# Odd attention scores as three fp32r products, and one LayerNorm's vectors loaded later

## The chip, the cores and the metric

The kernel runs on one core of a Trainium2 chip. The metric is the time of one execution on the device, in microseconds. TensorE (PE) multiplies, VectorE (DVE), ScalarE (ACT) and GpSimd (POOL) do the elementwise work, SyncE (SP) issues most transfers. Each engine takes its instructions in the order of its own queue and waits on semaphores for the others. Two formats of a matmul's operands occur here: fp32, whose two records in the trace are one instruction in the program, and fp32r, one record for each instruction, which rounds its operands.

## What is computed

A decoder trunk of two layers over 512 tokens of width 1024. Each layer is a mixer and a gated feed-forward network with a causal convolution of width 3, each followed by LayerNorm over `alpha * x + f(x)`. Layer 0 has the even mixer (16 heads of width 64), layer 1 the odd one (8 stick-breaking heads of width 128). The change touches the odd mixer:

```python
q, k, v = split_heads(h, w_qkv, 8, 128)          # h @ w_qkv
z = (q * 128 ** -0.5) @ k.T                      # per head, 128 queries at a time
z = where(kpos < t, z, -inf)
sp = max(z, 0) + log1p(exp(-abs(z)))
r = sum of sp from each key to the last          # reversed cumulative sum
out = exp(z - r) @ v
x = layer_norm(alpha * x + merge_heads(out) @ w_o, ln_mix_g, ln_mix_b)
```

## The kernel before

All large products run as three fp32r matmuls: an operand `w` is kept as a head `w_hi` (rounded to fp32r) and a rest `w_lo = w - w_hi`, and hi·hi, hi·lo and lo·hi are summed in PSUM. ACT writes the heads (L447 for the streamed weights), POOL (L311) and DVE the rests. Weights stream in 1 MB steps into two buffers `w_raw`.

The odd attention goes over eight positions, one head each (`odd_position` on PE, `odd_body` on ACT and DVE, `odd_position` on POOL). In position i the four query tiles j of 128 rows take the keys of tiles 0 to j, so scores are 128, 256, 384 and 512 columns wide. For a tile, PE writes z to bank 2 or 3 (`scores`, L1455), DVE masks the diagonal (L1048), ACT computes `log1p(exp(-abs(z)))` (L570 to L574), DVE adds the maximum, scans in reverse and subtracts (L1055, L1060, L1063: `break_stick`), ACT takes the exponential (L579), PE transposes (L1465), DVE (tiles 0 and 2, L977) or ACT (tiles 1 and 3, L482) copies the transposed weights out, and PE multiplies by the values (`weigh`, L1476).

Between these PE runs the projection of the next head's q and k, in its queue at places written by hand: `share = (10, 11, 15, 8, 2)` matmuls of 128x512 before tile 0's transposes, before tile 1's, before tile 2's, before tile 3's, and after the next position's first scores. 24 matmuls project one head's q into bank 0, 24 its k into bank 1. `EARLY` puts the first 12 of q for the position after the next behind those for the next one. So in a position i of 0 to 5 the first 36 matmuls finish q and k of head i+1, and what `fill(3)`, the share of 8 before tile 3's transposes, takes is the start of q of head i+2. It writes bank 0, in which q of head i+1 stood, and so waits:

```python
pe.wait_ge(a["q_ok" if l else "q_cp"], c + 2 * it)   # project_early, l = 1
```

`q_ok` counts the heads whose q has been read out of bank 0. Before the change ACT reads it in one copy (L592, scaled, into `qa`) and counts `q_ok`; the same for k (L598, `ka`, `k_ok`). PE waits for both again before the first scores of the next position. Positions 6 and 7 have no such early share.

DVE's body of a position ends with `turn_out(a, 2, ...)`, the copy L977 of tile 2's transposed weights. ACT loads gain and shift of a LayerNorm (`load_gain`, L451, two DMAs on its queue): for the even mixer right behind its attention, for the odd mixer at the end of layer 0's last LayerNorm, behind a wait for all of its rows. VectorE waits for them (`gb_full`) before the first row tile of the LayerNorm.

Of the kernel before, what the change touches and what calls it, by code (L numbers as in the profile page):

```python
# [22 lines left out]
F32 = mybir.dt.float32  # L23
F32R = mybir.dt.float32r
ACT = mybir.ActivationFunctionType
ALU = mybir.AluOpType

P = 128
S, D, DEPTH = 512, 1024, 2
# [3 lines left out]
NT = S // P  # L33
# [4 lines left out]
SB_SCALE = 128 ** -0.5  # L38
# [42 lines left out]
def build(nc, x_in, w_stream, ident_in, rope_in, mask_in, tri_in, conv_in, ln_in, out):  # L81
    ctx = ExitStack()
    with ctx:
        def sb(name, shape, dt=F32, stack=ctx):
            return stack.enter_context(nc.sbuf_tensor(name, shape, dt))
# [36 lines left out]
        with ExitStack() as st:  # L122
            v_all = sb("v_all", [P, NT, D], stack=st)
            v_pos = [sb(f"v_pos{s}", [P, NT, P], stack=st) for s in range(2)]
            probs_t = [sb(f"probs_t{h}", [P, NT, S], stack=st) for h in range(2)]
            with ExitStack() as ev:
                qa_hi = [sb(f"qa_hi{s}", [P, S], F32R, stack=ev) for s in range(2)]
                ka_hi = [sb(f"ka_hi{s}", [P, S], F32R, stack=ev) for s in range(2)]
            qa = [sb(f"qa{s}", [P, S], stack=st) for s in range(2)]
            ka = [sb(f"ka{s}", [P, S], stack=st) for s in range(2)]  # L130
            probs = [[sb(f"probs{h}{s}", [P, S], stack=st) for s in range(2)] for h in range(2)]
            with ExitStack() as ev:
                rope = sb("rope", [P, 2, S], stack=ev)
                masks = sb("masks", [P, 2, S], stack=ev)
                qc = sb("qc", [P, S], stack=ev)
                qs = sb("qs", [P, S], stack=ev)
                kc = sb("kc", [P, S], stack=ev)
                ks = sb("ks", [P, S], stack=ev)
                sm = sb("sm", [P, 2, 2, 4], stack=ev)
            with ExitStack() as od:  # L140
                soft = [sb(f"soft{s}", [P, S], stack=od) for s in range(2)]
                tri = sb("tri", [P, P], stack=od)
# [47 lines left out]
        class Phase:  # L190
# [4 lines left out]
            def __getitem__(self, n):  # L195
# [4 lines left out]
        V = [Phase(f"v{l}", "rows act dve") for l in range(DEPTH)]  # L200
        both = "q_mm q_ok k_ok s_mm p_ok t_mm tev_a tev_v v_pos pv ot_hi ot_lo "
        A = [Phase("a0", both + "q_cp k_cp q_sw k_sw q_m k_m s_rd ex rc p_ok1"),
             Phase("a1", both + "zm ab e1 ln sp sc rr")]
        N = [Phase(f"n{i}", "rows sum mean sq lv y0 va nt mulg xn") for i in range(2 * DEPTH)]
        T = [Phase(f"t{i}", "mm hi lo") for i in range(2 * DEPTH)]

# [235 lines left out]
        def _(act):  # L442
# [119 lines left out]
            def odd_body(b, c, it, dense, before, early):  # L562
                a = A[1]
                i = c + 2 * it

                def soft_part(j):
                    g, L = 4 * i + j, (j + 1) * P
                    e = soft[j % 2][:, 0:L]
                    act.wait_ge(a["zm"], g + 1)
                    act.activation(e, bank[2 + j % 2][:, 0:L], ACT.Abs).then_inc(a["ab"], 1)  # L570
                    act.wait_ge(a["ab"], g + 1)
                    act.activation(e, e, ACT.Exp, scale=-1.0).then_inc(a["e1"], 1)
                    act.wait_ge(a["e1"], g + 1)
                    act.activation(e, e, ACT.Ln, bias=1.0).then_inc(a["ln"], 1)  # L574

                def weight_part(j):
                    g, L = 4 * i + j, (j + 1) * P
                    act.wait_ge(a["rr"], g + 1)
                    act.activation(probs[0][j % 2][:, 0:L], probs[0][j % 2][:, 0:L], ACT.Exp).then_inc(a["p_ok"], 1)  # L579

                soft_part(0)
                soft_part(1)
                weight_part(0)
                heads(b + AT_QK + c + 2, it)
                if before:
                    out_heads(a, i - 1, (c - 1) % 2)
                weight_part(1)
                soft_part(2)
                turn_out(a, 1, 4 * i + 1, dense)
                if dense:  # L590
                    act.wait_ge(a["q_mm"], i + 2)
                    act.activation(qa[(c + 1) % 2][:, :], bank[0][:, :], ACT.Copy,  # L592
                                   scale=SB_SCALE).then_inc(a["q_ok"], 1)
                soft_part(3)
                weight_part(2)
                if dense:
                    act.wait_ge(w_used, b + AT_QK + i + 2)
                    act.activation(ka[(c + 1) % 2][:, :], bank[1][:, :], ACT.Copy).then_inc(a["k_ok"], 1)  # L598
                weight_part(3)
                turn_out(a, 3, 4 * i + 3, dense)  # L600

# [13 lines left out]
            for l in range(DEPTH):  # L615
                b = l * PER_LAYER

                if l == 0:
                    a = A[0]
                    query_copied(0)  # L620
                    act.wait_ge(w_used, b + 1)
                    act.activation(kc[:, :], bank[1][:, :], ACT.Copy).then_inc(a["k_cp"], 1)
                    body = even_body
                else:
                    a = A[1]

                    act.wait_ge(a["q_mm"], 1)
                    act.activation(qa[0][:, :], bank[0][:, :], ACT.Copy, scale=SB_SCALE).then_inc(a["q_ok"], 1)
                    act.wait_ge(w_used, b + 1)
                    act.activation(ka[0][:, :], bank[1][:, :], ACT.Copy).then_inc(a["k_ok"], 1)  # L630
                    act.dma_start(tri[:, :], tri_in).then_inc(tri_full, 16)
                    body = odd_body

# [19 lines left out]
                        body(b, 1, it, True, True, True)  # L653
                        body(b, 2, it, True, True, True)
                body(b, 7, 0, False, True, False)
                if l == 0:
                    load_gain(0)
                out_heads(A[l], 7, 1)

                for c in range(2):  # L660
# [3 lines left out]
                for i, after in ((2 * l, b + AT_O + 4), (2 * l + 1, b + PER_LAYER)):  # L664
# [167 lines left out]
                    else:  # L832
# [14 lines left out]
                            act.wait_ge(w_used, after)  # L847
                            act.activation(w_hi[s][:, part], w_raw[first % 2][:, 0:Q], ACT.Copy).then_inc(w["hi"], 1)
                        xt_heads(i + 1, 3)
                        if i % 2:  # L850
                            act.wait_ge(N[i]["xn"], NT)
                            load_gain(i + 1)


        @block.vector
        def _(dve):
# [130 lines left out]
            def even_body(c, it, dense, before, kind):  # L987
# [51 lines left out]
                if dense:  # L1039
                    k_rest(a, (c + 1) % 2, i + 1)  # L1040

            def odd_body(c, it, dense, before, kind):
                a, i = A[1], c + 2 * it

# [29 lines left out]
                break_stick(2)  # L1074
                break_stick(3)
                turn_out(a, 2, 0, 4, 4 * i + 2)

            dve.memset(v_all[:, 0, 0:P], 1.0).then_inc(warm_ready, 1)
            dve.memset(eps[:, :], 4 * EPS).then_inc(set_ready, 1)
# [9 lines left out]
            for l in range(DEPTH):  # L1089
                if l == 0:  # L1090
                    a = A[0]
                    dve.wait_ge(even_full, 32)
                    rope_k_cos(a, 0, 0)
                    rope_k_sin(a, 0, 0)
                    k_rest(a, 0, 0)
                    body = even_body
                else:
                    dve.wait_ge(tri_full, 16)
                    body = odd_body
                for t in range(NT):  # L1100
# [169 lines left out]
        def _(pe):  # L1270
# [171 lines left out]
            def odd_position(b, c, it, dense, early=False, filler=(), first=False):  # L1442
# [9 lines left out]
                        next(more, None)  # L1452

                def scores(j, p=par):
                    pe.matmul(bank[2 + j % 2][:, 0:(j + 1) * P], qa[p][:, j * P:(j + 1) * P],  # L1455
                              ka[p][:, 0:(j + 1) * P], start=True, stop=True).then_inc(a["s_mm"], 1)

                def turn(j):
                    pe.wait_ge(a["p_ok"], 4 * i + j + 1)
# [290 lines left out]
```

## Time and profile before

| | us |
|---|---|
| median of 3 runs | 1203.4 (1203.36 to 1203.89) |
| the profiled execution | 1203.59 |
| its span, first to last instruction | 1201.8 |
| PE busy | 1176.5 (98%) |
| DVE busy | 717.7 (60%) |
| ACT busy | 636.6 (53%) |
| POOL busy | 691.4 (58%) |

The odd attention lies between 676 and 809 us of the span; a position in its middle takes 16.52 us. A matmul's recorded duration includes its way through the array, and matmuls overlap: the time that one costs is the distance to the next. The chain of waits adds such distances up, and is the view to read them from.

### The profile page before, as it was taken

Reading aid. Unit: us, or ns where it says so; the run is one execution under the profiler, and the core shown is the slowest. Engines: PE = TensorE matmul, PEld = TensorE weight load, DVE = VectorE, ACT = ScalarE, POOL = GpSimd, SP = SyncE. Lnnn points to the kernel's source line nnn. Section 1 sums busy time; section 2 is a strip of 40 time slices with the busy share of each in tenths; the row PEclk is TensorE's granted clock in tenths of the full one; section 3 lists DMA queues with packets and bytes.
Section 4 is the critical chain, followed back from the end, with each engine's and each line's share of the span. In section 5 each row is a group of like instructions: output and inputs, shape, how many; then the busy total and the mean of one; then the engine's idle time right before and its main releaser. Section 6 shows DMA issues by size and latency. Waiting matters only on the chain.

```text
span 1201.8 us, 19742 instructions
## 1 busy us (share of the span) xinstructions
PE 1176.5 (98%) x7458; PEld 1038.3 (86%) x7458; DVE 717.7 (60%) x1376; ACT 636.6 (53%) x1105; POOL 691.4 (58%) x426
## 2 busy tenths in 40 slices
PE   9999998999999999999999999999999999999996
PEld 9877776789999999888788788878999999998885
DVE  2135556279988888421380455654998888872226
ACT  3256666355766666422242476753676666652223
POOL 4545555157877777654624333225687777765443
PEclk9999999999999999999999999999999999999999
DMA  6322212222232223422332211212122323243211
GB/s 252 124 76 74 97 62 96 73 103 71 106 105 105 105 105 105 143 103 105 103 107 101 77 54 52 70 70 105 36 106 105 105 105 105 105 140 105 105 70 70
DMA packets 20040, 117.42 MB, mean 98 GB/s; under 512 B 2448, under 2 KB 2832, under 8 KB 7568
## 3 DMA queue, kind: packets, MB, share of 16 engines
q1 hardware_dynamic: 18400, 112.21, 26.0%
q10 hardware_dynamic: 1584, 4.51, 1.2%
q8 instruction: 30, 0.49, 0.2%
q14 instruction: 26, 0.21, 0.1%
HBM read 110.41 MB, written 2.10 MB: 94 GB/s over the span
## 4 chain that ended last, share of the span: by engine, by line
PE 87%; DVE 7%; ACT 2%; POOL 2%; issue 1%; DVEq 0%; ACTq 0%
PE bank L1606 33%; PE bank L1302 29%; PE bank L1333 15%; POOL w_lo L311 2%; PE bank L1401 2%; PE bank L1476 1%; PE bank L1455 1%; PE bank L1415 1%; PE bank L1387 1%; PE bank L1277 1%; ACT w_hi L447 1%; PE bank L1465 1%; DVE ln_mul L893 1%; DVE x L873 1%; DVE xt_lo L861 1%
## 5 line engine op out<-in xcount | busy, mean ns | idle before, releaser
L311 POOL TENSOR_TENSOR w_lo<-w_raw,w_hi 128x1024 fp32r<-128x1024 f32 x116 | 298.4, 2591 | 319.4 <-ACT w_hi L447 277.6
L447 ACT ACTIVATE w_hi<-w_raw 128x2048 fp32r<-128x2048 f32 x55 | 105.1, 1911 | 199.7 <-PE bank L1302 192.5
L1606 PE MATMUL bank<-t_hi,w_hi 128*128 128x256 f32 x640 | 181.3, 283 | 2.6 <-DVE w_lo L1156 2.6
L1606 PE MATMUL bank<-t_lo,w_hi 128*128 128x256 f32 x640 | 181.1, 283 | 0.0
L1606 PE MATMUL bank<-t_hi,w_lo 128*128 128x256 f32 x640 | 181.1, 283 | 0.0
L405 POOL TENSOR_TENSOR w_lo<-w_raw,w_hi 128x512 fp32r<-128x512 f32 x120 | 156.1, 1302 | 20.3 <-ACT w_hi L698 19.7
L1302 PE MATMUL bank<-w_hi,a_hi 128*128 128x512 f32 x480 | 153.3, 394 | 1.8 <-POOL w_lo L311 1.2
L1302 PE MATMUL bank<-w_lo,a_hi 128*128 128x512 f32 x480 | 151.8, 391 | 0.0
L1302 PE MATMUL bank<-w_hi,a_lo 128*128 128x512 f32 x480 | 151.7, 390 | 0.0
L1333 PE MATMUL bank<-xt_hi,w_hi 128*128 128x512 f32 (+1 forms) x416 | 147.7, 355 | 2.4 <-ACT v_all L477 1.7
L405 POOL TENSOR_TENSOR w_lo<-qs_raw,w_hi 128x512 fp32r<-128x512 f32 x80 | 104.2, 1302 | 72.7 <-ACT w_hi L698 72.7
L1333 PE MATMUL bank<-xt_lo,w_hi 128*128 128x512 f32 (+1 forms) x416 | 145.1, 349 | 0.0
L1333 PE MATMUL bank<-xt_hi,w_lo 128*128 128x512 f32 (+1 forms) x416 | 143.4, 345 | 0.0
L1235 DVE TENSOR_TENSOR a_lo<-h_all,a_hi 128x1024 fp32r<-128x1024 f32 x22 | 49.9, 2267 | 155.2 <-ACT a_hi L672 155.2
L1606 PE MATMUL bank<-xt_hi,w_hi 128*128 128x256 f32 x480 | 135.8, 283 | 0.0
L1606 PE MATMUL bank<-xt_lo,w_hi 128*128 128x256 f32 x480 | 135.8, 283 | 0.0
L1606 PE MATMUL bank<-xt_hi,w_lo 128*128 128x256 f32 x480 | 135.8, 283 | 0.0
L1606 PEld LDWEIGHTS bank<-t_hi,w_hi 128*128 128x128 f32 x640 | 122.9, 192 | 3.0 <-DVE w_lo L1156 3.0
L1606 PEld LDWEIGHTS bank<-t_lo,w_hi 128*128 128x128 f32 x640 | 122.9, 192 | 0.0
L1606 PEld LDWEIGHTS bank<-t_hi,w_lo 128*128 128x128 f32 x640 | 122.9, 192 | 0.0
L1302 PEld LDWEIGHTS bank<-w_hi,a_hi 128*128 128x128 f32 x480 | 88.5, 188 | 23.6 <-POOL w_lo L311 4.7
L1302 PEld LDWEIGHTS bank<-w_lo,a_hi 128*128 128x128 f32 x480 | 90.1, 188 | 19.3 <-issue 0.5
(142 smaller groups left out, 2515.1 us busy)
## 6 DMA issues: line engine op xcount, KB each, us to landing
w_raw<-w_stream SPq DMA_DIRECT2D x97, 1024.0 KB, 4.8
x<-x_in SPq DMA_DIRECT2D x4, 512.0 KB, 7.2
qs<-qc SPq DMA_DIRECT2D x16, 128.0 KB, 2.0
ks<-kc SPq DMA_DIRECT2D x16, 128.0 KB, 2.0
gain<-ln_in ACTq DMA_DIRECT2D x4, 512.0 KB, 5.0
shift<-ln_in ACTq DMA_DIRECT2D x4, 512.0 KB, 6.0
out<-x SPq DMA_DIRECT2D x3, 512.0 KB, 2.6
w_raw<-w_stream SPq DMA_DIRECT2D x2, 512.0 KB, 6.1
```

Source lines behind the costliest of these rows:

```text
L311: pool.tensor_tensor(w_lo[slot(c)][:, part], w_raw[s][:, part], w_hi[slot(c)][:, part].bitcast(F32), ALU.subtract).then_inc(lo_ready, 1)
L405: pool.tensor_tensor(w_lo[s][:, part], src, w_hi[s][:, part].bitcast(F32), ALU.subtract).then_inc(w["lo_p"], 1)
L447: act.activation(w_hi[slot(c)][:, :], w_raw[c % 2][:, :], ACT.Copy).then_inc(hi_ready, 2)
L861: dve.tensor_tensor(xt_lo[:, 4 * g:4 * g + 4, t * P:(t + 1) * P], bank[2 * t + g][:, :].rearrange("p (k q) -> p k q", k=4), part.bitcast(F ...
L873: dve.scalar_tensor_tensor(out=x[:, t, g * HALF:(g + 1) * HALF], in0=x[:, t, g * HALF:(g + 1) * HALF], scalar=ALPHA, in1=bank[2 * t + g][: ...
L893: dve.scalar_tensor_tensor(out=product(i, t), in0=x[:, t, :], scalar=stat[:, t, 2:3], in1=gain[:, :], op0=ALU.add, op1=ALU.mult).then_inc( ...
L1235: dve.tensor_tensor(a_lo[:, k:k + 2, :], h_all[:, bass.ds(2 * j, 2), :], a_hi[:, k:k + 2, :].bitcast(F32), ALU.subtract).then_inc(DN[l]["a ...
L1277: mm = pe.transpose(bank[2 * t + k // 4][:, (k % 4) * P:(k % 4 + 1) * P], x[:, t, k * P:(k + 1) * P], ident[:, :])
L1302: mm = pe.matmul(bank[2 * t + g][:, :], lhs, w[s][:, u * UNIT + g * HALF:u * UNIT + (g + 1) * HALF], start=first and n == 0, stop=end and ...
L1333: mm = pe.matmul(out_bank[:, tok], w, m, start=n == 0, stop=n == len(todo) - 1)
L1401: mm = pe.transpose(bank[4 + h][:, m * P:(m + 1) * P], probs[h][qi % 2][:, k * P:(k + 1) * P], ident[:, :])
L1606: mm = pe.matmul(out, lhs[s][:, at], rhs[:, k, :], start=(k, v) == (0, 0), stop=(k, v) == (3, 2))
```

## The change

Odd scores are computed as the even ones: heads and rests of q and k, three fp32r matmuls into the same bank. ACT now writes the heads `qa_hi`, `ka_hi` and counts `q_hi`, `k_hi`; DVE computes the rests from the banks and the heads and counts `q_ok`, `k_ok`. The two DVE instructions stand at the end of `odd_body`. The odd mixer's `load_gain` moves behind the odd attention. PE's shares, `EARLY` and the places of its waits stay as they are.

```diff
@@ scalar: odd_body, and the same before position 0
-                    act.activation(qa[(c + 1) % 2][:, :], bank[0][:, :], ACT.Copy,
-                                   scale=SB_SCALE).then_inc(a["q_ok"], 1)
+                    act.activation(qa_hi[(c + 1) % 2][:, :], bank[0][:, :], ACT.Copy,
+                                   scale=SB_SCALE).then_inc(a["q_hi"], 1)
-                    act.activation(ka[(c + 1) % 2][:, :], bank[1][:, :], ACT.Copy).then_inc(a["k_ok"], 1)
+                    act.activation(ka_hi[(c + 1) % 2][:, :], bank[1][:, :], ACT.Copy).then_inc(a["k_hi"], 1)
@@ scalar: after body(b, 7, 0, False, True, False)
-                if l == 0:
-                    load_gain(0)
+                load_gain(2 * l)
@@ scalar: end of a LayerNorm
-                        if i % 2:
-                            act.wait_ge(N[i]["xn"], NT)
-                            load_gain(i + 1)
@@ vector
+            def q_rest(a, s, i):
+                dve.wait_ge(a["q_hi"], i + 1)
+                dve.scalar_tensor_tensor(out=qa_lo[s][:, :], in0=bank[0][:, :], scalar=SB_SCALE,
+                                         in1=qa_hi[s][:, :].bitcast(F32), op0=ALU.mult,
+                                         op1=ALU.subtract).then_inc(a["q_ok"], 1)
+            def k_rest_odd(a, s, i):
+                dve.wait_ge(a["k_hi"], i + 1)
+                dve.tensor_tensor(ka_lo[s][:, :], bank[1][:, :], ka_hi[s][:, :].bitcast(F32),
+                                  ALU.subtract).then_inc(a["k_ok"], 1)
@@ vector: odd_body (the same two calls stand before position 0 too)
                 turn_out(a, 2, 0, 4, 4 * i + 2)
+                if dense:
+                    q_rest(a, (c + 1) % 2, i + 1)
+                    k_rest_odd(a, (c + 1) % 2, i + 1)
@@ tensor: odd_position
                 def scores(j, p=par):
-                    pe.matmul(bank[2 + j % 2][:, 0:(j + 1) * P], qa[p][:, j * P:(j + 1) * P],
-                              ka[p][:, 0:(j + 1) * P], start=True, stop=True).then_inc(a["s_mm"], 1)
+                    for n, (q, k) in enumerate(((qa_hi, ka_hi), (qa_hi, ka_lo), (qa_lo, ka_hi))):
+                        mm = pe.matmul(bank[2 + j % 2][:, 0:(j + 1) * P], q[p][:, j * P:(j + 1) * P],
+                                       k[p][:, 0:(j + 1) * P], start=n == 0, stop=n == 2)
+                    mm.then_inc(a["s_mm"], 1)
```

How the queues stand. First VectorE, the end of an odd position inside the loop (`a1_` names the odd attention's semaphores; line numbers of after are its own). Before:

```order
646 L1055 SCALAR_TENSOR_TENSOR soft<-bank,soft 128x512 [waits a1_ln]
647 L1060 SCALAR_TENSOR_TENSOR probs<-soft 128x512 [waits a1_sp]
648 L1063 TENSOR_TENSOR probs<-bank,probs 128x512 [waits a1_sc]
649 L977 COPY probs_t<-bank 128x3x128 [waits a1_t_mm]
650 L1046 ISA
651 L1048 TENSOR_TENSOR bank<-bank,tri 128x128 [waits a1_s_mm]
```

The same place after:

```order
650 L1059 SCALAR_TENSOR_TENSOR soft<-bank,soft 128x512 [waits a1_ln]
651 L1064 SCALAR_TENSOR_TENSOR probs<-soft 128x512 [waits a1_sp]
652 L1067 TENSOR_TENSOR probs<-bank,probs 128x512 [waits a1_sc]
653 L970 COPY probs_t<-bank 128x3x128 [waits a1_t_mm]
654 L1036 REGISTER_ALU
655 L1037 SCALAR_TENSOR_TENSOR qa_lo<-bank,qa_hi 128x512 [waits a1_q_hi]
656 L1043 TENSOR_TENSOR ka_lo<-bank,ka_hi 128x512 [waits a1_k_hi]
657 L1050 ISA
```

Two rests now stand between the copy of tile 2's weights and the next position's first mask. Second TensorE, from tile 2's transposes to the start of `fill(3)`, before:

```order
1786 L1459 REGISTER_ALU
1787 L1461 ISA [waits a1_p_ok]
1788 L1465 MATMUL bank<-ident,probs 128x128 [waits a1_tev_v]
1789 L1465 MATMUL bank<-ident,probs 128x128 x2
1790 L1360 REGISTER_ALU
1791 L1332 ISA [waits a1_q_ok]
1792 L1333 MATMUL bank<-xt_hi,w_hi 128x512 [waits lo_ready]
```

and after:

```order
1802 L1470 REGISTER_ALU
1803 L1472 ISA [waits a1_p_ok]
1804 L1476 MATMUL bank<-ident,probs 128x128 [waits a1_tev_v]
1805 L1476 MATMUL bank<-ident,probs 128x128 x2
1806 L1369 REGISTER_ALU
1807 L1341 ISA [waits a1_q_ok]
1808 L1342 MATMUL bank<-xt_hi,w_hi 128x512 [waits lo_ready]
```

Nothing moved here: the wait for `a1_q_ok` stands where it stood, but another engine counts it. Third TensorE, the first scores of the next position, before:

```order
1807 L1474 REGISTER_ALU
1808 L1476 MATMUL bank<-probs_t,v_pos 128x128 [waits a1_tev_v]
1809 L1476 MATMUL bank<-probs_t,v_pos 128x128 x2
1810 L1455 MATMUL bank<-ka,qa 128x128 [waits a1_k_ok,a1_q_ok]
1811 L1455 MATMUL bank<-ka,qa 128x256
```

and after:

```order
1826 L1465 MATMUL bank<-ka_hi,qa_hi 128x128 [waits a1_k_ok,a1_q_ok]
1827 L1465 MATMUL bank<-ka_lo,qa_hi 128x128
1828 L1465 MATMUL bank<-ka_hi,qa_lo 128x128
1829 L1465 MATMUL bank<-ka_hi,qa_hi 128x256
1830 L1465 MATMUL bank<-ka_lo,qa_hi 128x256
1831 L1465 MATMUL bank<-ka_hi,qa_lo 128x256
```

Each score has become three matmuls at the same place.

## Rows read from the trace of the kernel before

**Rows 1.** Page, part 1: busy time, share, instructions of each engine.

```profile
PE 1176.5 (98%) x7458; PEld 1038.3 (86%) x7458; DVE 717.7 (60%) x1376; ACT 636.6 (53%) x1105; POOL 691.4 (58%) x426
```

**Rows 2.** Busy time by stretch, odd attention: PE, PEld, DVE, ACT, POOL, clock, DMA.

```profile
705.00:720.00 15.00, 15.00 (x80) 12.30 (x79) 8.15 (x19) 10.53 (x22) 5.50 (x3) 1.00 0.09 26
```

**Rows 3.** Chain that ended last, positions 0 to 2: start us, us, what.

```profile
688.29 1.86 PE bank L1333 x8
...
700.19 0.86 PE bank L1455 x2
701.05 3.43 PE bank L1333 x15
...
704.81 1.85 PE bank L1333 x8
...
708.44 0.66 PE bank L1455 x4
...
713.30 0.65 PE bank L1455 x2
...
716.71 0.86 PE bank L1455 x2
```

**Rows 4.** Timeline of VectorE, positions 0 and 1: start us, us, line, what.

```profile
689.70 0.55 DVE L977 COPY probs_t<-bank 128x384 f32<-128x384 f32 x1
...
703.39 0.69 DVE L1055 SCALAR_TENSOR_TENSOR soft<-bank,soft 128x512 f32<-128x512 f32 x1
704.11 1.22 DVE L1060 TENSOR_TENSOR_SCAN probs<-soft 128x512 f32<-128x512 f32 x1
705.37 0.69 DVE L1063 TENSOR_TENSOR probs<-bank,probs 128x512 f32<-128x512 f32 x1
705.98 0.55 DVE L977 COPY probs_t<-bank 128x384 f32<-128x384 f32 x1
```

**Rows 5.** Timeline of ScalarE, the same position: the copies of q and k.

```profile
700.51 0.59 ACT L592 ACTIVATE qa<-bank 128x512 f32<-128x512 f32 x1
...
704.52 0.60 ACT L598 ACTIVATE ka<-bank 128x512 f32<-128x512 f32 x1 [0.53 <-PE bank L1333]
```

**Rows 6.** Chain, fp32r matmuls elsewhere: 256-wide (L1606), even scores (L1387).

```profile
299.97 40.08 PE bank L1606 x334
...
75.36 0.88 PE bank L1387 x12
...
80.52 0.72 PE bank L1387 x6
...
85.07 0.89 PE bank L1387 x6
```

**Rows 7.** Timeline of PE, even scores 128 wide: two heads at once.

```profile
75.45 0.27 PE L1387 MATMUL bank<-ka_lo,qa_hi 64*128 64x128 f32 x2
75.57 0.27 PE L1387 MATMUL bank<-ka_hi,qa_lo 64*128 64x128 f32 x2
```

**Rows 8.** Chain, end of position 6 and first scores of position 7.

```profile
788.70 0.64 ACT probs L579
...
789.39 0.66 PE bank L1465 x4
...
790.71 0.66 PE bank L1455 x4
```

**Rows 9.** Busy time by stretch as in rows 2: an idle PE, twice.

```profile
788.20:789.20 1.00, 0.00 (x0) 0.00 (x0) 0.93 (x2) 0.50 (x1) 0.15 (x1) 1.00 0.03 8
1194.00:1196.00 2.00, 0.00 (x0) 0.00 (x0) 1.96 (x5) 1.02 (x1) 0.00 (x0) 1.00 0.63 260
...
1197.00:1198.00 1.00, 0.00 (x0) 0.00 (x0) 0.90 (x5) 0.00 (x0) 0.00 (x0) 0.62 1.01 410
```

**Rows 10.** Timeline of PE: the last matmul of the kernel.

```profile
1192.73 0.39 PE L1302 MATMUL bank<-w_hi,a_lo 128*128 128x512 f32 x1
```

**Rows 11.** Timeline of ScalarE: the load that moves, and its new place.

```profile
624.62 0.34 ACTq L451 DMA_DIRECT2D gain<-ln_in  x1
...
630.58 0.60 ACT L628 ACTIVATE qa<-bank 128x512 f32<-128x512 f32 x1 [4.88 <-PE bank L1333]
...
808.62 0.60 ACT L488 ACTIVATE a_hi<-bank 128x512 fp32r<-128x512 f32 x1 [1.90 <-PE bank L1476]
...
829.72 1.15 ACT L463 ACTIVATE ln_junk<-x,stat 128x1024 f32<-128x1024 f32 x1 [1.95 <-DVE stat L880]
```

**Rows 12.** Page, part 6: issues, KB each, median us to landing.

```profile
shift<-ln_in ACTq DMA_DIRECT2D x4, 512.0 KB, 6.0
```

More of the change, by code:

```diff
@@ L125, in build @@
             probs_t = [sb(f"probs_t{h}", [P, NT, S], stack=st) for h in range(2)]
[L126 to L130, printed above, removed]
+            qa_hi = [sb(f"qa_hi{s}", [P, S], F32R, stack=st) for s in range(2)]
+            ka_hi = [sb(f"ka_hi{s}", [P, S], F32R, stack=st) for s in range(2)]
             probs = [[sb(f"probs{h}{s}", [P, S], stack=st) for s in range(2)] for h in range(2)]
@@ L202, in build @@
         A = [Phase("a0", both + "q_cp k_cp q_sw k_sw q_m k_m s_rd ex rc p_ok1"),
-             Phase("a1", both + "zm ab e1 ln sp sc rr")]
+             Phase("a1", both + "q_hi k_hi zm ab e1 ln sp sc rr")]
         N = [Phase(f"n{i}", "rows sum mean sq lv y0 va nt mulg xn") for i in range(2 * DEPTH)]
@@ L627, in _ @@
                     act.wait_ge(a["q_mm"], 1)
-                    act.activation(qa[0][:, :], bank[0][:, :], ACT.Copy, scale=SB_SCALE).then_inc(a["q_ok"], 1)
+                    act.activation(qa_hi[0][:, :], bank[0][:, :], ACT.Copy, scale=SB_SCALE).then_inc(a["q_hi"], 1)
                     act.wait_ge(w_used, b + 1)
-                    act.activation(ka[0][:, :], bank[1][:, :], ACT.Copy).then_inc(a["k_ok"], 1)
+                    act.activation(ka_hi[0][:, :], bank[1][:, :], ACT.Copy).then_inc(a["k_hi"], 1)
                     act.dma_start(tri[:, :], tri_in).then_inc(tri_full, 16)
@@ L1097, in _ @@
                 else:
+                    q_rest(A[1], 0, 0)
+                    k_rest_odd(A[1], 0, 0)
                     dve.wait_ge(tri_full, 16)
```

## Prediction

> **What bounds the kernel now.** I read the page's busy times first: PE is busy for 98% of the span, no other engine above 60% [rows 1]. In the odd attention it is the same: 15.00 of 15.00 us busy on PE, 8.15 on DVE, 10.53 on ACT, at full clock [rows 2]. Then the chain of waits, for the order of events inside a position: from one start of the 512-wide score to the next, 700.19 to 716.71, is 16.52 us, and the chain never leaves PE [rows 3]. So a microsecond saved on PE is a microsecond, and so is one for which PE has to stand. Last the timelines of DVE and ACT over the same stretch, since the change hands DVE work on which PE waits.
>
> **Part 1, the scores themselves.** Eight positions with four scores each. Before, 128 and 256 wide take 0.66 us together, 384 wide 0.65, 512 wide 0.86 [rows 3]. After, each is three fp32r passes with weights of their own. A 512-wide pass costs 3.43 / 15 = 0.229 us [rows 3], so 0.69 for three; a 256-wide one 40.08 / 334 = 0.120 [rows 6], so 0.36. For 384 I take the middle, 0.174, so 0.52 (an estimate from these two). At 128 wide the nearest rows are the even scores, where two starts stand 0.12 us apart at most [rows 7], so 0.35. The differences are +0.05 (128 and 256 together), -0.13 (384) and -0.17 (512): -0.25 per position.
>
> The bound on the dear side is the even attention, where whole groups of such passes, on half the array's rows for two heads at once, cost 0.88 (128 and 256), 0.72 (384) and 0.89 (512) [rows 6]. That is 0.57 per position more than my values, 4.6 us over eight. I take the cheap values because the odd scores use all 128 rows like the projections beside them, and those run at 0.229 with no gap at the change of kind [rows 3]. On the cheap side nothing goes below zero for the 128-wide passes: at most 0.35 less per position, 2.8 us in all, which nothing in the rows suggests.
>
> **Part 2, the rests on DVE, and who waits.** Before, q of the next head leaves bank 0 with ACT's copy, done at 701.10, and k with the copy done at 705.12 [rows 5]. PE asks for q before the first matmul of `fill(3)`, which starts at 704.81 [rows 3]: 3.7 us to spare, so the wait costs nothing. After, the count comes from DVE's rest, and that stands last in DVE's queue for the position. DVE is then in the second half of its chain for tiles 2 and 3: L1055 at 703.39, the scan at 704.11, the subtraction at 705.37, and the copy of tile 2's weights at 705.98, done at 706.53 [rows 4]. The rest of q is one instruction over 128x512 with a PSUM operand; the row of the same kind is L1055 at 0.69 us [rows 4], with a small gap 0.70. It ends at 707.23, and with 0.04 us for the signal (the gap between the end of L579, 789.34, and the transposes at 789.39 [rows 8]) PE is released at 707.27. All of this hangs on the 512-wide score, which is 0.17 shorter: 707.10. PE stands from 704.64 to 707.10, **2.46 us**, where it stood for nothing.
>
> Per position, at the start of `fill(3)`: 707.10 - 704.81 = +2.29. A PE that restarts also loses its overlap: four transposes after a wait take 0.66 us [rows 8], while three in the flow take 0.33 (701.05 + 3.43 = 704.48 to 704.81 [rows 3]), 0.11 each; so +0.2. To this come -0.13 for tile 2's score and +0.05 for the first two. Sum **+2.41** per position.
>
> Does anything take this up again? From `fill(3)` round to the next 512-wide score, 704.81 to 716.71, the chain has PE alone [rows 3], and from that score's end to the rest of q it is DVE without a pause. The two halves make one loop with nothing loose in it. The wait sits in positions 0 to 5. In position 0, `fill(3)` starts at 688.29 [rows 3] and the copy ends at 690.25 [rows 4]: 690.25 + 0.74 - 0.17 - 688.29 = 2.53, with 0.2 - 0.13 + 0.05: +2.65. So 5 x 2.41 + 2.65 = **+14.7 us**.
>
> The rest of k ends 0.7 us after that of q, about 707.8. PE needs it for the next first scores, which come 3.6 us after the start of `fill(3)` (704.81 to 708.44 [rows 3]): covered. Behind the two rests in DVE's queue is only the next position's first mask, which waits for those scores anyway. Position 6 has no `fill(3)` share. There the copy ends some 0.45 us after L579 starts (706.53 against 706.06, the end of L1063, in position 1 [rows 4]; L579 starts right behind it), so the rest of k ends at 788.70 + 0.45 + 1.40 = 790.55, and the first scores start at 790.71 [rows 8]: no wait, by 0.16. Should it fail, it costs some tenths once. Positions 6 and 7 then keep the gain of part 1: -0.25 and -0.30 (position 7 has no first scores to pay for), and the very first scores cost +0.05. Sum **-0.5 us**.
>
> ACT's copies keep their places; only their output's type changes. The rests ahead of position 0 fall where DVE has finished the LayerNorm and PE works on the values: ACT's q copy there is at 630.58 [rows 11], more than 40 us before the first scores. I cost them at nothing.
>
> **Part 3, the moved load.** Its removal saves nothing: ACT idles 4.88 us between those two DMA issues (624.62) and its next copy at 630.58, and that one waits for PE [rows 11]. In the new place ACT idles 1.90 us before L488 at 808.62 [rows 11], and the two issues take 0.34 us and a little more. The vectors land 6 us after issue [rows 12], say at 815, and the LayerNorm works from 829.7 [rows 11]: 15 us of cover. SP's queue is not involved. Nothing, then; if the weights' stream were held up by 1 MB more beside it, a microsecond at most.
>
> **Sum.** 14.7 - 0.5 + 0 = +14.2 us. The profiled execution took 1203.6, 0.2 above the median of 1203.4; its span plus 1.8. On the median: **1217.6 us**.
>
> **The rivals.**
>
> *The clock falls at each stop.* A PE that stands 2.46 us, six times, may be given the lower of its two levels, 1.2 GHz instead of 2.4. The rows bound it from both sides: idle from 788.2 at the latest [rows 9] to 789.39 [rows 8], with the clock at 1.00 [rows 9], and after the kernel's last matmul (ended at 1193.12 [rows 10]) it was still 1.00 to 1196 and averaged 0.62 from 1197 to 1198 [rows 9], so it fell some 4 us after. If the 3.63 us of PE work from `fill(3)` to the next scores then ran at half speed, each stop would cost 3.6 more: 1239 if all six do, 1225 if two do. [...] Chance 0.11.
>
> *The passes cost what the even groups cost.* As worked out in part 1, 4.6 us more: 1222.2. For it speaks that these are the only scores of this form in the trace; against it, that they use half the rows and two tiles of the array. Chance 0.07.
>
> *PE does not stand (the other side).* If the rest of q were done before PE asks, the kernel would only have part 1: 8 x -0.25 = -2.0, 1201.4. The point is whether DVE delivers it by 704.6, so 2.6 us earlier than I find. DVE idles before the mask at 701.09 and q has its head at 701.10 [rows 5], so there would be room ahead of tile 3's chain; but an engine takes its instructions in order, and they stand behind the copy. Only if I misread which head's count `fill(3)` asks for could this come true. Chance 0.04.
>
> **How the numbers follow.** The forecast has 0.78, rivals 0.11, 0.07 and 0.04. Its own spread: without the restart's 0.2 per stop -1.2; the rest as short as the copy L977 (0.55) -0.8; the dear side of a rest that meets POOL's traffic or waits a little more, +2. That is 1215.5 to 1219.6. The range reaches over the dear passes and a clock that falls in one stop or two, and a little below for a shorter tail: 1214.5 to 1224. About 0.2% (2.4 us) is what a measurement of this kernel can tell from no change. Faster 0.03, same 0.01, slower 0.96.
>
> **What would show it.** In the profile after: PE idle before a line L1342 or its wait, released by DVE's `qa_lo`, six times, some 2.4 us each, 14 to 15 us in all; a middle position of 18.9 us instead of 16.5; DVE's rests 0.7 us each; scores of 0.52 and 0.69 us for 384 and 512 columns in the chain; clock 1.00 throughout; no wait for `gb_full`. It would be wrong if PE showed no such wait, if the granted clock in 676 to 825 were below 1, or if score passes showed gaps between them.

## The result and the profile after

The kernel after takes **1229.2 us** (1228.17 to 1230.82), the kernel before 1203.4 beside it (1203.26 to 1203.89): a ratio of 1.0215, 95% interval 1.0197 to 1.0233. The forecast was 1217.6 with a range to 1224. The direction was right, the size was not: the loss is 25.8 us where 14.2 were worked out. The profiled execution took 1229.2, its span is 1227.4. One run of the kernel with the share moved (the last experiment but one) took 4094.11 us and is left out of its numbers.

The page of after, its parts 1 (against [rows 1]), 2 and 5:

```profile
PE 1185.8 (97%) x7490; PEld 1049.5 (86%) x7490; DVE 729.6 (59%) x1392; ACT 637.2 (52%) x1105; POOL 692.3 (56%) x426
...
PEclk9999999999999999999999989899999999999998
...
L1342 PE MATMUL bank<-xt_hi,w_hi 128*128 128x512 f32 (+1 forms) x416 | 147.0, 353 | 17.1 <-DVE qa_lo L1037 14.7
```

Two things are new: PE waits 14.7 us for DVE's `qa_lo`, and two slices in the odd attention show a granted clock below 9 tenths. PE's waits there, as engine, line, waited for, us in total, times, longest:

```profile
PE bank L1342 <- DVE qa_lo L1037: 14.7, 6, 2.5
PE bank L1476 <- ACT probs L576: 3.0, 4, 1.3
```

So the stop is there, six times, 2.45 us each in the mean (2.36 to 2.54), as forecast. The chain of position 1 shows it (start us, us, what), against [rows 3]:

```profile
704.61 0.72 PE bank L1465 x3
...
710.24 0.55 DVE probs_t L970
710.79 0.61 DVE qa_lo L1037
711.40 0.13 issue
711.53 2.96 PE bank L1342 x8
714.48 1.28 PE bank L1487 x6
...
716.35 0.67 PE bank L1487 x6
```

Behind the stop, `fill(3)`'s eight matmuls take 2.96 us instead of 1.85 [rows 3], and six matmuls of L1487 take 1.28 where the next six take 0.67. The busy times by stretch, with the columns of [rows 2], say why:

```profile
708.50:711.00 2.50, 0.58 (x5) 0.27 (x3) 2.47 (x4) 1.23 (x2) 1.07 (x1) 1.00 0.69 288
711.50:712.50 1.00, 0.97 (x4) 0.85 (x5) 0.48 (x1) 0.00 (x0) 0.00 (x0) 1.00 0.00 0
712.52:715.93 3.41, 3.41 (x13) 2.97 (x12) 0.00 (x0) 0.00 (x0) 0.00 (x0) 0.50 0.00 0
716.00:720.00 4.00, 4.00 (x30) 3.73 (x29) 1.76 (x6) 2.80 (x9) 0.00 (x0) 1.00 0.00 0
```

The clock stays full through this stop, falls to half (1.2 of 2.4 GHz) 1.0 us after PE is back at work, stays there for 3.41 us of uninterrupted work, and returns. The same 3.41 us come once in each of positions 0 to 5, at 692.04, 712.52, 733.0, 753.48, 773.96 and 794.44. These falls are 20.48 us apart each, the stops some 20.6: so the fall comes 1.09 us after PE's return in position 0 and only 0.57 us after it in position 5. It doesn't follow the stop at a fixed distance.

**Where the 25.6 us of span went.** From the first 512-wide score to the seventh it is 124.9 us where it was 99.9: +24.9. Nothing else in the attention is longer: -0.3 ahead of that stretch, and no change behind it (0.15 of the 0.3 stands already at the first odd score, so ahead of the attention). A position in the middle has grown from 16.52 us to 20.60. The remaining +1.0 lies in the odd mixer's LayerNorm (further below). The experiments give the clock's share.

### The profile page after: what moved, and what is told of

It reads as the page before. It is cut to its first block, busy times and chain, and to the rows that moved or that the text cites. A ratio compares the mean times of both kernels' runs of the same rounds, so it can differ in the third digit from the quotient of the medians.

```text
span 1227.4 us, 19828 instructions
## 1 busy us (share of the span) xinstructions
PE 1185.8 (97%) x7490; PEld 1049.5 (86%) x7490; DVE 729.6 (59%) x1392; ACT 637.2 (52%) x1105; POOL 692.3 (56%) x426
## 3 DMA queue, kind: packets, MB, share of 16 engines
q1 hardware_dynamic: 18400, 112.21, 25.6%
## 4 chain that ended last, share of the span: by engine, by line
PE 83%; DVE 10%; ACT 2%; POOL 2%; issue 2%; DVEq 0%; ACTq 0%
PE bank L1617 32%; PE bank L1311 28%; PE bank L1342 13%; POOL w_lo L308 2%; PE bank L1487 2%; PE bank L1410 2%; DVE probs L1064 2%; PE bank L1424 1%; PE bank L1396 1%; PE bank L1465 1%; DVE ln_mul L886 1%; DVE x L909 1%; ACT w_hi L444 1%; PE bank L1286 1%; DVE x L866 1%
## 5 line engine op out<-in xcount | busy, mean ns | idle before, releaser
L1342 PE MATMUL bank<-xt_hi,w_hi 128*128 128x512 f32 (+1 forms) x416 | 147.0, 353 | 17.1 <-DVE qa_lo L1037 14.7
```

What stands on the lines that cost most here:

```text
L1342: mm = pe.matmul(out_bank[:, tok], w, m, start=n == 0, stop=n == len(todo) - 1)
```

## The experiments

All edits are to the kernel after, except where "before" is named.

**The stop alone, without fp32r scores.** Before, with one edit: q leaves bank 0 by a DVE copy at the end of `odd_body`, where after has the rests. The scores stay fp32.

```diff
@@ scalar, odd_body
-                    act.activation(qa[(c + 1) % 2][:, :], bank[0][:, :], ACT.Copy, scale=SB_SCALE)...
@@ vector, end of odd_body
+                    dve.wait_ge(a["q_mm"], i + 2)
+                    dve.tensor_scalar(qa[(c + 1) % 2][:, :], bank[0][:, :], SB_SCALE, None,
+                                      ALU.mult).then_inc(a["q_ok"], 1)
```

> The kernel before with one thing changed: q leaves bank 0 by a copy on VectorE at the end of its body (where the change puts q's rest) instead of a copy on ScalarE. Scores stay fp32, no rests, the load in its old place. It makes the stop without the new arithmetic. Stop: 706.53 + 0.6 + 0.04 - 704.81 = 2.36 us, with the restart 2.5, in six positions 15 us; with the fall of the clock as in the changed kernel (1.6 each) 24.9: 1228 us. If the fall needs the fp32r passes: 1218.5 us. If the stop is not what costs the time at all: 1203.4 us.

Measured: 1228.6 (1226.2 to 1229.0), ratio 1.0197 [1.0181, 1.0213]. PE's wait, a stretch with a fall and one without:

```profile
PE bank L1333 <- DVE qa L1075: 14.8, 6, 2.6
...
700.00:720.00 20.00, 17.54 (x81) 13.93 (x81) 9.82 (x19) 10.30 (x19) 5.83 (x3) 0.91 0.15 53
757.90:795.30 37.40, 32.57 (x169) 26.39 (x168) 20.45 (x40) 22.08 (x42) 11.76 (x6) 1.00 0.16 56
754.45:754.80 0.35, 0.00 (x0) 0.00 (x0) 0.22 (x1) 0.00 (x0) 0.00 (x0) 0.50 0.00 0
```

The clock fell in five positions of six here, though all six stops are 2.37 to 2.57 us long. The last row shows one of the falls inside a stop: it came at 754.41, PE was back at 754.81. From the first 512-wide score to the seventh it is 123.9 us, 23.9 more than before, where the whole change costs 24.9 with one fall more. (Its span is 25.4 us longer; 1.6 of them stand already at the first odd score, with a fall in the even attention, see the load below.) So the place of q's last reader makes the stop and the falls by itself; fp32r scores are not needed for either.

**PE kept at work in the stop.** Dummy matmuls of 128x512 into a free bank, behind tile 2's transposes and ahead of the wait for `q_ok`, in positions 0 to 5: ten, five or three of them (0.229 us each, so the stop left to PE is about 0.2, 1.3 or 1.8 us). The rest of q comes when it came.

```diff
                 for j in range(NT):
+                    if j == 3 and early:
+                        pe.wait_ge(a["tev_a"], 2 * i + 1)
+                        for _ in range(10):              # 5, 3
+                            pe.matmul(bank[5][:, :], xt_hi[:, 0, 0:P], xt_hi[:, 0, :], start=True, stop=True)
                     fill(share[j])
```

> The changed kernel with ten more matmuls of 128x512 (2.3 us) into an unused bank just before the wait for q_ok in positions 0 to 5, results unused: TensorE is busy for most of the time that it would stand, and q arrives no earlier. If the stop itself makes the clock fall and that costs 1.7 us in each of six positions, the clock stays at 1.00 and the time is 1229.2 - 10.2 = 1219.0 us, less some tenths per position for the restart, so 1218 to 1219. If the fall has another cause (the passes in fp32r, the longer position), it stays at 1229 us or more.

> The changed kernel with five idle-filling matmuls of 128x512 before the wait for q_ok instead of the ten of x3_warm: q arrives when it did, and TensorE stands about 1.3 us instead of 2.46 (with ten it was about 0.2). If the length of the stop decides, the clock stays as in x3_warm: 1219 to 1220 us. If a stop of 1.3 us is enough for a fall: 1229 us.

> As x6_warm5 with three idle-filling matmuls: TensorE stands about 1.8 us instead of 1.4 (five of them) or 2.5 (none). q_ok arrives at the same time in all of them, so only the clock can differ. At 1.4 us it fell in none of six positions, at 2.0 in five, at 2.5 in six. If the length of the stop decides: a number in between, 1219 us plus 1.6 for each fall, 1220 to 1229.

Measured: ten give 1219.7 (1218.42 to 1220.54), ratio 1.0138 [1.0123, 1.0154]; five 1218.7 (1218.45 to 1219.06), 1.0121 [1.0106, 1.0137]; three 1221.2 (1221.12 to 1222.45), 1.0151 [1.0135, 1.0167]. Of five dummies, PE's wait, a stretch, and the chain of position 1:

```profile
PE bank L1342 <- DVE qa_lo L1037: 7.7, 6, 1.4
...
700.00:720.00 20.00, 18.71 (x102) 15.70 (x101) 11.59 (x24) 12.41 (x25) 6.88 (x4) 1.00 0.14 52
...
709.32 0.61 DVE qa_lo L1037
...
710.06 2.10 PE bank L1342 x8
```

No fall in the odd attention with ten or five. A position takes 18.99 us, and `fill(3)` 2.10 instead of 1.85: that is the 0.2 us of a restart. With three dummies one position of six had a fall, here the first (0.91), not the next:

```profile
PE bank L1342 <- DVE qa_lo L1037: 10.5, 6, 1.8
...
680.00:700.00 20.00, 17.09 (x85) 14.20 (x84) 11.03 (x20) 10.36 (x22) 5.39 (x3) 0.91 0.14 53
700.00:720.00 20.00, 18.25 (x99) 15.34 (x98) 11.82 (x23) 12.61 (x23) 5.86 (x3) 1.00 0.14 53
```

Useless work makes the kernel 10 us faster. The clock's share of the loss is 6 x (20.60 - 18.99) = 9.7 us by the traces. The medians differ by 1229.2 - 1218.7 = 10.5; in them is also most of the 1.0 us behind the attention, which the kernels with five and ten dummies don't have (`ln_mul` 1.69 and 1.61, see below). Most of the rest, 14.7 us, is the wait that DVE's order makes, which the dummies leave as it is.

**A shorter stop.** The rest of q ahead of DVE's copy of tile 2's weights instead of behind it.

```diff
@@ vector, odd_body
+                if dense:
+                    q_rest(a, (c + 1) % 2, i + 1)
                 turn_out(a, 2, 0, 4, 4 * i + 2)
                 if dense:
-                    q_rest(a, (c + 1) % 2, i + 1)
                     k_rest_odd(a, (c + 1) % 2, i + 1)
```

> The changed kernel with q's rest ahead of the copy of tile 2's weights on VectorE, nothing else: TensorE should stand 0.55 us less per position, 1.9 us instead of 2.46. If the clock falls at a stop of that length as it does at 2.46: 1229.2 - 6 x 0.55 = 1225.9 us. If 1.9 us is short enough for the clock to stay: another 6 x 1.6 less, 1216.3 us. In between if it falls in some positions only.

Measured: 1224.6 (1223.43 to 1226.08), ratio 1.0167 [1.0151, 1.0182]. The stop went down by 0.45 us, most of the copy's 0.55, and the clock still fell in five positions of six:

```profile
PE bank L1343 <- DVE qa_lo L1037: 12.0, 6, 2.1
```

A position takes 20.1 us with a fall and 18.5 without: 1.6 once more. Together, for the profiled executions:

| stop of PE, us | 2.45 | 2.5 (fp32 scores) | 2.0 | 1.8 | 1.3 | 0.2 or less |
|---|---|---|---|---|---|---|
| clock falls in 6 positions | 6 | 5 | 5 | 1 | 0 | 0 |

These are one execution each, and lengths in the mean; the one fall with three dummies came at the longest of its stops, 1.84 us (the others 1.65 to 1.75). Longer stops go with more falls, but length alone doesn't decide: one position of six escaped at 2.46 us and one at 2.0. The even attention shows the same (at the load below). A rival stands untested: that the moment at which a stop lies matters as well. No run moved the stops without changing their length.

**No stop at all.** ACT writes q's head ahead of `turn_out(1)` instead of behind it, and DVE the rest of q ahead of the last tile's mask, so before its chain for tiles 2 and 3. The rest of k stays last.

```diff
@@ scalar, odd_body: the four lines of the copy of q's head move up
-                turn_out(a, 1, 4 * i + 1, dense)
                 if dense:
                     act.wait_ge(a["q_mm"], i + 2)
                     ...
+                turn_out(a, 1, 4 * i + 1, dense)
@@ vector, odd_body
+                if dense:
+                    q_rest(a, (c + 1) % 2, i + 1)
                 mask_diagonal(3)
...
                 if dense:
-                    q_rest(a, (c + 1) % 2, i + 1)
                     k_rest_odd(a, (c + 1) % 2, i + 1)
```

> The changed kernel with q's head ahead of the copy of tile 1's weights on ScalarE and q's rest ahead of the mask of tile 3 on VectorE, where that engine idled; k's rest stays last. Theory (TensorE stands at q_ok because the rest of q is last in VectorE's queue, and the clock falls because TensorE stands): no stop, clock 1.00 throughout, and only the cheaper scores are left: 1203.4 - 2.0 = 1201.4 us, or 1202.4 if the 1 us behind the attention stays. Rival (the three passes themselves or the two rests cost the time, wherever they stand): well above 1205 us.

Measured: 1203.1 (1202.88 to 1204.89), ratio 0.9998 [0.9989, 1.0007]. A stretch, then the chain from one 512-wide score to the next:

```profile
700.00:720.00 20.00, 20.00 (x108) 17.00 (x107) 14.19 (x28) 14.23 (x27) 7.32 (x4) 1.00 0.20 65
...
716.22 0.71 PE bank L1466 x3
...
720.69 1.85 PE bank L1343 x8
...
724.32 0.69 PE bank L1466 x6
...
729.22 0.53 PE bank L1466 x3
...
732.52 0.71 PE bank L1466 x3
```

In these positions the chain has PE alone again, a position takes 16.30 us, and the whole 25.8 us are gone with two instructions put elsewhere. The expected 1201.4 or 1202.4 us was not reached. The attention starts 0.5 us earlier than before, as in other runs, and ends 1.4 us earlier, so it is itself 1.0 us shorter where 2.0 were expected (position 0 alone is 0.3 longer); some 0.7 is given back in the LayerNorm behind it. As a kernel it is no faster than before, so nothing beat the kernel before here.

**The passes alone.** After without the rests: all three passes read the heads, which stand at once behind ACT's copies, and the LayerNorm's vectors are loaded in the old place. What it leaves out is the rests' part of the scores, so its output is coarser.

```diff
@@ vector: the calls of q_rest and k_rest_odd are removed; ACT's copies count q_ok and k_ok
@@ tensor
-                    for n, (q, k) in enumerate(((qa_hi, ka_hi), (qa_hi, ka_lo), (qa_lo, ka_hi))):
+                    for n, (q, k) in enumerate(((qa_hi, ka_hi), (qa_hi, ka_hi), (qa_hi, ka_hi))):
```

> Scores in three fp32r passes, but without the rests: the two passes with a rest take the heads again, so the scores are wrong in value and VectorE has nothing added; q_ok and k_ok are counted by ScalarE as before, and the load is in its old place. It measures the price of the passes alone. Forecast's term: -0.25 us per position, 8 positions: 1201.4 us. Rival (passes as dear as the even attention's groups, +0.3 us per position): 1206 us.

Measured: 1202.7 (1202.1 to 1204.48), ratio 0.9993 [0.9984, 1.0002]. Its chain, a 512-wide score, the two first ones, a 384-wide:

```profile
717.82 0.70 PE bank L1464 x3
...
725.90 0.69 PE bank L1464 x6
...
730.81 0.53 PE bank L1464 x3
```

0.70, 0.69 and 0.53, forecast 0.69, 0.71 and 0.52; a position is 0.27 us shorter than before, and the attention as a whole 1.45. The time is 1.3 us above the expected 1201.4: 0.7 us lie in the LayerNorm behind the attention (below), 0.5 in the attention's short gain. The profiled execution was one of the slow ones of the eleven, 1204.28, with a fall of the clock in the even attention.

**The load alone.** Before, with `load_gain(2 * l)` behind each attention and the old place gone.

> The kernel before with the moved load alone: the odd mixer's gain and shift are loaded behind the odd attention, scores stay fp32. In the changed kernel the stretch behind the attention is 1.0 us longer than before (TensorE's lead over the kernel before grows from 24.65 to 25.63 us between its matmuls at 836 and 873 us). If the moved 1 MB causes that, this kernel takes 1204.4 us. If it is something else (a weight transfer that took 4.8 us instead of 3.5, with an instruction fetch in its middle), it takes 1203.4 us. The forecast's term for the load was nothing.

Measured: 1204.0 (1203.28 to 1205.42), ratio 1.0007 [0.9998, 1.0016]: nothing that can be told, between the two expectations of 1204.4 and 1203.4. The profiled execution, 1203.28 and so its fastest, has a fall of the clock in the even attention, which neither part touches, 0.4 us behind a stop of 1.70 us:

```profile
201.62 1.12 PE L1397 MATMUL bank<-ident,probs 128*128 128x128 f32 x6 [1.70 <-ACT probs L524]
...
200.00:220.00 20.00, 16.38 (x96) 11.30 (x96) 11.98 (x48) 10.86 (x31) 6.17 (x3) 0.91 0.27 102
```

That stop is in all 13 kernels, and the clock fell at it in three of the profiles (this one, five dummies, shorter work in position 6). PE's next stop there is 2.1 us long where the first brought no fall, in ten kernels, and the clock fell at it in three (shorter stop, the stop alone, the passes alone). In the kernel before it fell at neither; its second stop, and the work behind it:

```profile
209.31:211.39 2.08, 0.00 (x0) 0.03 (x1) 1.72 (x4) 0.92 (x3) 1.18 (x1) 1.00 0.00 0
211.50:214.90 3.40, 3.40 (x21) 2.59 (x20) 1.84 (x9) 2.08 (x7) 0.00 (x0) 1.00 0.83 306
```

A fall at the first stop costs little, since the second is then 1.15 to 1.34 us instead of 2.1. After one at the second the odd attention starts 1.4 to 1.7 us later than before. That falls make the higher of the times, here and of the kernel before (up to 1205.95), is likely, but those executions weren't profiled.

**The +1.0 us behind the attention.** ScalarE's timeline in the odd mixer's LayerNorm, before and after: the copy of the weights' heads waits for their transfer, 4.30 us before, 5.78 after.

```profile
825.84 1.92 ACT L447 ACTIVATE w_hi<-w_raw 128x2048 fp32r<-128x2048 f32 x1 [4.30 <-DMA w_raw<-w_stream]
```

```profile
851.97 1.93 ACT L444 ACTIVATE w_hi<-w_raw 128x2048 fp32r<-128x2048 f32 x1 [5.78 <-DMA w_raw<-w_stream]
```

Then POOL's rests come later too. In both kernels DVE's first `ln_mul` lies beside them, but before, the first of the two rests has 0.5 us left when it starts, and after 2.0, and it takes twice as long; before, then after:

```profile
827.84 2.41 POOL L311 TENSOR_TENSOR w_lo<-w_raw,w_hi 128x1024 fp32r<-128x1024 f32 x1 [1.48 <-ACT w_hi L447]
829.72 1.62 DVE L893 SCALAR_TENSOR_TENSOR ln_mul<-x,stat,gain 128x1024 f32<-128x1024 f32 x1
```

```profile
853.98 2.41 POOL L308 TENSOR_TENSOR w_lo<-w_raw,w_hi 128x1024 fp32r<-128x1024 f32 x1 [2.96 <-ACT w_hi L444]
854.37 3.10 DVE L886 SCALAR_TENSOR_TENSOR ln_mul<-x,stat,gain 128x1024 f32<-128x1024 f32 x1
```

In all 13 kernels `ln_mul` ends 1.08 to 1.09 us after the end of that first rest, whether it had started 0.4 or 2.0 us before that end; with no rest beside it, it takes 1.28. So it hardly advances beside the first rest, and the time of that rest is what counts.

The moved load isn't the cause (it is issued 15 us before this transfer): moved alone it brings none of this (`ln_mul` 1.50), and the passes alone, with the load in its old place, bring +0.7 (`ln_mul` 2.85). What goes with it is an instruction fetch in the same microseconds, here the second queue of after between 846 and 852 us:

```profile
q1 hardware_dynamic: 145, 1.06, 56.2%
q8 instruction: 1, 0.02, 0.9%
```

In the eight kernels in which the fetch lies in this 1 MB transfer, the transfer takes 4.4 to 4.8 us; in the five others, before among them, 3.5 to 3.6. To move the fetch on purpose I put 24 waits that were long met among PE's value matmuls of the kernel without a stop:

```diff
+                        if l == 1 and n % 6 == 3:
+                            pe.wait_ge(warm_ready, 1)
+                            pe.wait_ge(ident_full, 16)
```

> x2_q_early with 24 more instructions in TensorE's program, waits on semaphores that were reached long ago, among the value matmuls of the odd layer. In x2_q_early an instruction fetch (820.6 to 822.2 us) falls into the first of the two weight transfers ahead of the odd mixer's LayerNorm; that transfer takes 4.6 instead of 3.5 us, GpSimd's rests start 1.3 us later and lie beside VectorE's first LayerNorm multiplication (2.85 instead of 1.6 us), and TensorE loses 0.8 us. 24 instructions are some 2.8 us of TensorE's program: the fetch should fall ahead of the transfer, and the time to 1202.3 us. If the fetch is not TensorE's or not the cause: 1203.1 us, as x2_q_early.

Measured: 1203.0 (1202.68 to 1204.62), ratio 0.9995; the fetch still lies in the transfer (4.76 us, `ln_mul` 2.92). The experiment missed its aim. That the fetch is the cause remains a coincidence seen in every kernel, not shown by moving it.

**Taking away the share on which the stop sits.** `share = (10, 11, 15, 0, 10)`: `fill(3)` takes nothing, and its eight matmuls come behind the next position's first scores.

> The changed kernel with the early share of 8 matmuls moved from ahead of tile 3's transposes to behind the next position's first scores, share (10, 11, 15, 0, 10); VectorE's order stays. The wait for q_ok then stands where q_ok has long been reached. What is late next is the last exponential: TensorE stands some 1.1 us for it, as in position 6 (1.3 us), and restarts at 0.2. By rows of the kernel before a position takes 16.52 - 0.25 + 1.1 + 0.2 = 17.6 us, with no fall of the clock at a stop this short: 1203.4 - 2.0 + 6 x 1.3 = 1209.2 us, up to 1210.2. If the clock falls at stops of 1.1 us too: 1219.

Measured: 1212.55 (1212.49 to 1213.89), ratio 1.0081 [1.0063, 1.0100], a position 17.80 us.

```profile
PE bank L1476 <- ACT probs L576: 10.9, 10, 1.5
...
708.38 0.66 PE bank L1476 x4
...
710.39 2.29 PE bank L1342 x10
```

The stop for `qa_lo` is gone, and PE now stands for ACT's last exponential, since nothing is left to cover it. These stops are no longer than 1.5 us, and the clock stayed at 1.00. The sum I had put down for it was 3 us low: the stretch of the six positions is 8.4 us longer than before where 6.3 were put down (a stop of 1.3 us, not 1.1, and 0.6 more in position 0), and the 1.0 us behind the attention was not in it.

**Shorter work in position 6** of the kernel without a stop, `share = (10, 5, 15, 6, 0)` there.

> x2_q_early with another share in position 6, (10, 5, 15, 6, 0) instead of (10, 11, 15, 8, 2): six projection matmuls go from ahead of tile 1's transposes to ahead of tile 3's, where TensorE waits 1.3 us for the last exponential. ScalarE's copy of k stands ahead of that exponential and waits for the end of the same matmuls, so half of the wait should stay: 0.6 us less than x2_q_early, 1202.5 us. If the copy of k holds the exponential up for as long as the wait was, nothing is won: 1203.1 us.

Measured: 1203.3 (1202.86 to 1205.23), ratio 1.0001, as the second of the two expectations has it. PE's wait of 1.3 us for the last exponential went down to 0.54, but a new one of 0.83 stands ahead of tile 2's transposes, which have less work before them; together that is as much as before. ACT's copy of k's head holds the last exponential up, which is why 0.54 us stay (the chain of waits, position 6, then PE's timeline):

```profile
787.05 0.60 ACT ka_hi L595
787.64 0.53 ACT probs L576
```

```profile
785.07 0.55 PE L1477 MATMUL bank<-ident,probs 128*128 128x128 f32 x3 [0.83 <-ACT probs L576]
```

## Why the prediction was wrong, step by step

- **What bounds the kernel:** right. Six pauses of PE, 2.45 us each, went into the time in full.
- **Part 1, the passes:** right per position. -0.25 us forecast, -0.27 measured by themselves, -0.22 in the kernel without a stop. Over the whole attention the gain was 1.45 and 1.0 us, less than the 2.0 of eight positions. The rival by which they cost what the even groups cost (+4.6 us) fell.
- **Part 2, the stop:** right in its place, number and length. 6 x 2.46 forecast, 14.7 us measured; the rest of q 0.68 us (0.69 and a gap of 0.01); the restart 0.25 (0.2); a position without a fall 18.99 us, forecast 16.52 + 2.41 = 18.93. The rest of k made no wait in position 6. In the length there is some luck: PE started 0.13 us after the rest's end where 0.04 was put down (the two times that the prediction names are 0.05 apart), and the rest began 0.08 us before the recorded end of the copy.
- **The clock: this step failed.** The forecast put the fall of the clock at nothing. Between two bounds, 1.3 us of idling with no fall [rows 8, 9] and some 4 us after the last matmul with one [rows 9, 10], I put a stop of 2.46 with the first, at a chance of 0.11 for the other. The second bound was read wrongly: it gives the time from a stop's start to the fall, not how long PE has to stand. In after the fall comes 3.4 us after the last matmul ahead of the stop (which ended at 709.09 in position 1), when PE has been back for 1.0 us; over all positions it is 2.9 to 3.6 us, and in the stop alone it can be 2.1. So the 4 us said nothing against 2.46. The rows of before had nearer stops that I didn't use, 1.70 and 2.09 us in the even attention, both at full clock; they would have made me surer, and wrong too, since the clock fell at the same two stops in other kernels. What the runs show: falls at 2.4 to 2.5 us in eleven of twelve positions, at about 2.0 in five of six, at 1.7 to 1.8 in one of six, none at 1.2 to 1.5. The prediction's own sign of being wrong, a granted clock below 1 between 676 and 825 us, came true. The Trainium skill, "TensorE: Matmul & The Clock Gate", section "Why this matters for your kernels", advises against idle gaps between bursts of matmuls, but only against longer ones than any stop here. Taken as a limit this is too lax here: the clock fell at all six stops of 2.36 to 2.54 us.
- **The rival's price:** 3.6 us per stop was too high, measured 1.6. I let all 3.63 us of work from `fill(3)` to the next scores run at half speed, which is 7.3 us at the half level. In the trace it lasts 3.41 us, in which 1.7 us of work get done, so 1.7 are lost. With the measured price the rival gives 1217.6 + 9.7 = 1227.3. The range held falls in two stops only.
- **Part 3, the load:** right, nothing that can be told (1204.0 against 1203.4 by itself). But 1.0 us behind the attention wasn't foreseen, for another reason.
- **PE does not stand:** fell, as read from the order of DVE's queue. Its price was 2.0 us of gain; the kernel without a stop gained 0.3 by the medians, for the reasons given there.

**The sum again:** 14.2 forecast, 9.7 for the clock, 1.0 for the LayerNorm, and 0.8 in small parts: position 0 cost 0.4 more than its 2.65 and a fall, the next four 0.06 each and the sixth 0.07 less, and the stretches ahead of these positions and behind them are 0.3 shorter instead of 0.5. That makes 25.7, and the spans differ by 25.6.

## What to carry to other kernels

When an operand's last reader moves to another engine, look for who waits to write its buffer again, not only for who reads the result: here eight matmuls of the head after the next stood behind it, and two instructions placed earlier in two queues were worth 26 us. A stop of TensorE can have two prices, the stop and a stretch at half clock, and the second may show only behind the stop; at the stops of 2 us and more here it nearly always came. Put both in the sum. Where the order can't be mended, useless matmuls in the stop can win back the second.

## What the runs showed of the hardware

- At stops of 1.7 to 2.6 us the granted clock fell 1.9 to 3.6 us after TensorE's last matmul, so between 0.4 us before its return (the stop alone) and 1.5 us after it (three dummies). It then stood at half for 3.41 us in every such fall of the 13 profiles; in the odd attention each cost 1.6 us, and 1.4 to 1.5 in the stop alone, where part of some lay in the stop.
- In the odd attention, once per position: stops of 1.2 to 1.5 us lowered it never (six with five dummies, seven with the share moved), 1.65 to 1.84 us once in six, 1.9 to 2.1 us in five of six, 2.4 to 2.6 us in eleven of twelve. In the even attention a stop of 1.7 us lowered it in 3 of 13 profiles and one of 2.1 us in 3 of 10. Length alone doesn't decide; what else does isn't shown.
- An fp32r pass of 128 columns costs as much as one of 256, 0.11 to 0.12 us from start to start (TensorE's timeline in after, below; 0.17 once, at the first of 256). Three passes are cheaper than one fp32 matmul at 384 and 512 columns and slightly dearer at 128 and 256 together (0.69 against 0.66).
- A 1 MB transfer took 4.4 to 4.8 us with an instruction fetch in it and 3.5 to 3.6 without, which goes together and isn't shown as cause.
- DVE's 128x1024 `ln_mul` ended 1.08 to 1.09 us after the end of POOL's first rest beside it in all 13 kernels, and so took from 1.5 to 3.1 us, against 1.28 with no rest beside it.

```profile
717.02 0.28 PE L1465 MATMUL bank<-ka_hi,qa_lo 128*128 128x128 f32 x1
717.14 0.33 PE L1465 MATMUL bank<-ka_hi,qa_hi 128*128 128x256 f32 x1
717.31 0.28 PE L1465 MATMUL bank<-ka_lo,qa_hi 128*128 128x256 f32 x1
717.42 0.28 PE L1465 MATMUL bank<-ka_hi,qa_lo 128*128 128x256 f32 x1
```

The third column is what a matmul's record spans, with its way through the array; the distances of the first column are the cost.
